# State space's in weights ahead of its out weights, turned between row units; the last product's rests moved from GpSimd to VectorE

## The chip, the cores and the metric

The kernel runs on one NeuronCore of a Trainium2 chip. The metric is the device time of one execution in microseconds (us). Engines are named as the profile names them: PE (TensorE, with PEld for its weight loads), DVE (VectorE), ACT (ScalarE), POOL (GpSimd) and SP (SyncE, which here only issues DMAs). SBUF is the on-chip memory, PSUM the memory that PE writes; DVE and ACT read PSUM, POOL does not.

## What is computed

Two transformer blocks on one sequence of 512 tokens with 1024 features, in fp32. The first block mixes three branches (sparse attention, a gated recurrence, a latent attention) and ends in a feed-forward layer. The second block, in which the change lies, is this, cut to what matters:

```python
def s5_mixer(u, a_re, a_im, log_dt, b_re, b_im, c_re, c_im, d_skip):
    lam_bar = exp(complex(a_re, a_im) * dt)
    b_bar = ((lam_bar - 1) / lam)[..., None] * complex(b_re, b_im)
    # per group of 16 features: 64 complex states
    #   s[t] = lam_bar * s[t-1] + b_bar @ u[t];  y[t] = real(c @ s[t])
    return y + d_skip * u

def hybrid_layer(x, c, ...):
    h = rms_norm(x, norm_g) * (1 + scale) + shift
    proj = h @ w_in          # q, compressed/selected/window keys and values, z_a, gates, u, z_s
    attn = nsa_attention(...) * silu(z_a)        # 8 heads, three branches
    y = gelu(s5_mixer(u, ...))
    y = y * sigmoid(y @ glu_w + glu_b)
    mix = concatenate([attn, y * silu(z_s)]) @ w_out
    return x + gate * mix
```

## The kernel before

One program drives five engines, each with its own list of instructions, kept together by counting semaphores. The order on each engine is the order in which the code writes it; nothing is scheduled later. Names such as `at("in weights 0 3")` are values of such a counter.

**Weights** come from HBM in chunks of up to 128x2048 through `ring`, a ring of four slots. SP issues the loads in a fixed order, each behind the wait that its slot has been used. A *unit* is one output tile of a projection: a feature unit has eight products of 128x512 (each shows as two records), a row unit eight products with 256 columns, or 24 in the last four of the 20 row units. A unit writes one of three PSUM banks (`gemm_bank`), from which ACT copies it (`drain`); PE may take a bank again once the unit three places before was drained. The state space's products go to two other banks (`turn_bank`, `turn0` and `turn1`), which DVE reads.

**Precise products** (`triple`) split each operand into a rounded head and a rest. ACT makes the head of a weight piece (`weight_heads`, into `heads`, four pieces of 128x1024), and another engine subtracts it to get the rest (`ring_r`, in place). In the whole kernel this is DVE (`weight_rests`), but for the last product, `w_out` of the second block (`WOUT2`), it is POOL: its rests of the weights, of the state space's output (`split ssm`) and of three of four key blocks of the attention output (`split late 0` to `2`); DVE makes only the last, `split late 3`.

**State space.** The scan over 512 tokens is done in steps of four tokens (`STEP`), for 16 tiles j of 128 states. Two matrices, real and imaginary (z), hold the loaded weights and their multiples by the decay: `BK` (in weights, lives in `tiles`) and `CK` (out weights, in `rows` and `heads`). DVE folds a factor into `CK` (`fold_out_weights`, 6 instructions), makes four further out weights (24), three in weights (18), clears `TOEP` and makes the diagonal of `d_skip` in the place of the scratch tile `wi`; then `ssm matrices` is reached. PE then multiplies in and out weights (L1106, L1107, four banks, `out weights`), and transposes `BK` in eight groups of four (L1114), which ACT drains back over it as `BT` (`in weights z b4`). ACT also issues three DMAs that spread `TOEP` (L1667), and makes sines and cosines (`waves`, L1653 to L1655). For each of four blocks b4, PE multiplies `BT` with the input `U4` (L1125, `full bu`), DVE turns, scans and turns back (L2386 is the scan) and says `states`, and PE makes y (L1139 to L1141), to which ACT applies the gelu (L1659). Between these steps PE runs `SIDE[b4]` units. SP rearranges `u` into `U4` by 16 DMAs, and y by 16 DMAs (L623) behind `y_done`; the latter stand in its list between the loads of the second and third compression chunks (`cmp_k1`, `cmp_k2`), and the load of `cmp_k1` waits until the second last pair of feature units has been used. The gated linear product (`glu`) waits for them.

**The pair loop.** 64 items of attention (2 branches x 4 query blocks x 8 heads), two to a round p of 32. In round p PE makes the scores of pair p (L1244, L1247), the sums of pair p - 2 (L1270) and the transposes of pair p - 1 (L1256). DVE takes the maximum of pair p (L2578), copies the transposed probabilities of pair p - 1 to `probs` or `probsT` (L1810), and in every second round scales the sums (L2547, L2552). ACT makes the exponentials (L1706). The query blocks have 128, 256, 384 and 512 keys, so rounds 12 to 15 and 28 to 31 are the long ones. After the loop come the halves of the last product (`wide_half`, L707), of which the first ones stand between the last sums, and then four full tiles.

## Time and profile before

| what | value |
|---|---|
| median of three runs | 1583.59 us (1580.87 to 1591.41) |
| profiled execution | 1581.13 us |
| its span, first to last instruction | 1579.3 us |
| mean granted clock of PE | 0.945 of full |
| PE busy | 1423.6 us (90%) |
| DVE busy | 955.5 us (60%) |
| ACT busy | 525.4 us (33%) |
| POOL busy | 83.4 us (5%) |

The profile is of one execution. Its own time is 1.8 us longer than its span, which is what lies around the instructions. Times in the rows are counted from the start of the span. PE's records overlap a little, since products are pipelined, so the distance from start to start is the better measure of what one costs.

### The profile page before, as it was taken

How to read it: one execution, taken by the hardware profiler on the slowest of the kernel's cores; microseconds unless marked ns; L12 is line 12 of the kernel's file. 1: busy time of each engine (PE TensorE's matmuls, PEld its weight loads, DVE VectorE, ACT ScalarE, POOL GpSimd, SP SyncE). 2: the span in 40 equal slices, each digit the busy share in tenths (PEclk: the TensorE clock that was granted, in tenths of full speed). 3: DMA queues.
4: the chain of work that ended last, by engine and by line, in shares of the span. 5: the costliest groups of instructions: out<-in, count | busy, mean ns of one | idle time of the engine just before them, and what ended most of it. 6: DMA issues, size and time to landing. Idle time of an engine off the chain costs nothing.

```text
span 1579.3 us, 18880 instructions
## 1 busy us (share of the span) xinstructions
PE 1423.6 (90%) x7109; PEld 1105.4 (70%) x7110; DVE 955.5 (60%) x1606; ACT 525.4 (33%) x840; POOL 83.4 (5%) x67
## 2 busy tenths in 40 slices
PE   5998888896989877899899999999798999988898
PEld 4758788785567645787688888888557954565576
DVE  6249767676166777774545655533393738868761
ACT  5247332331323554233333333423223031214421
POOL 0000000000000350000000000000000002001212
PEclk9999999997989979899899999999898999989999
DMA  5112111121222120452134444223421122430001
GB/s 229 71 41 93 67 41 54 61 90 47 86 107 81 48 71 14 150 212 92 70 111 183 161 159 155 72 91 110 134 57 63 54 80 72 168 107 1 1 1 54
DMA packets 39882, 140.52 MB, mean 89 GB/s; under 512 B 13040, under 2 KB 17520, under 8 KB 27248
## 3 DMA queue, kind: packets, MB, share of 16 engines
q1 hardware_dynamic: 34608, 130.53, 23.5%
q10 hardware_dynamic: 5184, 8.78, 1.5%
q8 instruction: 57, 0.93, 0.2%
q14 instruction: 33, 0.27, 0.1%
HBM read 128.42 MB, written 8.39 MB: 87 GB/s over the span
## 4 chain that ended last, share of the span: by engine, by line
PE 54%; DVE 4%; ACT 1%; issue 1%; ACTq 0%; DVEq 0%
PE turn L707 24%; PE score L692 7%; PE score L707 7%; PE sum L692 4%; PE sum L707 2%; PE sum L1270 2%; PE score L1244 1%; PE sum L1152 1%; PE score L1152 1%; PE turn L1256 1%; PE turn L829 1%; DVE stat L2578 1%; PE turn L1125 1%; DVE probs L1810 0%; PE score L1206 0%
## 5 line engine op out<-in xcount | busy, mean ns | idle before, releaser
L1852 DVE TENSOR_TENSOR ring_r<-ring,heads_r 128x1024 fp32r<-128x1024 f32 (+3 forms) x153 | 176.3, 1152 | 220.5 <-ACT heads_r L1378 185.0
L1378 ACT ACTIVATE heads_r<-ring 128x1024 fp32r<-128x1024 f32 (+3 forms) x161 | 161.8, 1005 | 250.7 <-DMA ring<-wstream 114.3
L707 PE MATMUL score<-h_sb_r,heads_r 128*128 128x512 f32 x408 | 163.9, 402 | 0.0
L707 PE MATMUL turn<-tiles_r,heads_r 128*128 128x512 f32 x368 | 144.6, 393 | 0.0
L707 PE MATMUL turn<-h_sb_r,heads_r 128*128 128x512 f32 x336 | 132.1, 393 | 8.1 <-DVE ring_r L1852 8.1
L707 PE MATMUL turn<-wide_r,heads_r 128*128 128x512 f32 x312 | 121.9, 391 | 0.0
L707 PE MATMUL turn<-wide_r,ring_r 128*128 128x512 f32 x312 | 121.6, 390 | 0.0
L707 PE MATMUL score<-x_sb_r,heads_r 128*128 128x512 f32 x256 | 109.3, 427 | 8.2 <-DVE ring_r L1852 5.7
L707 PE MATMUL score<-x_sb_r,ring_r 128*128 128x512 f32 x256 | 103.5, 404 | 0.0
L707 PEld LDWEIGHTS score<-h_sb_r,heads_r 128*128 128x128 f32 x408 | 79.5, 195 | 15.1 <-issue 0.5
L707 PEld LDWEIGHTS turn<-tiles_r,heads_r 128*128 128x128 f32 x368 | 70.1, 190 | 14.5
L707 PEld LDWEIGHTS turn<-h_sb_r,heads_r 128*128 128x128 f32 x336 | 63.8, 190 | 21.7 <-issue 8.4
L2630 POOL TENSOR_TENSOR stat<-stat,cst 128x4 f32<-128x4 f32 (+4 forms) x7 | 16.1, 2294 | 1179.7 <-DVE stat L1855 803.9
L707 PE MATMUL sum<-h_sb_r,heads_r 128*128 128x512 f32 x168 | 67.6, 402 | 0.0
L707 PEld LDWEIGHTS turn<-wide_r,ring_r 128*128 128x128 f32 x312 | 58.8, 189 | 12.4
L707 PEld LDWEIGHTS turn<-wide_r,heads_r 128*128 128x128 f32 x312 | 58.9, 189 | 12.2
L707 PEld LDWEIGHTS score<-x_sb_r,heads_r 128*128 128x128 f32 x256 | 50.7, 198 | 22.8 <-issue 10.0
L707 PE MATMUL turn<-h_sb_r,ring_r 128*128 128x512 f32 x160 | 63.0, 394 | 0.0
L707 PEld LDWEIGHTS score<-x_sb_r,ring_r 128*128 128x128 f32 x256 | 50.5, 197 | 11.3
L1706 ACT ACTIVATE tiles<-score,stat 128x128 f32<-128x128 f32 (+3 forms) x64 | 33.7, 527 | 73.3 <-issue 63.2
L692 PE MATMUL score<-h_sb,ring 128*128 128x512 f32 x128 | 55.8, 592 | 0.0
L1347 ACT ACTIVATE tiles<-score 128x512 f32<-128x512 f32 x39 | 24.3, 622 | 91.6 <-PE score L692 41.9
(401 smaller groups left out, 2963.4 us busy)
## 6 DMA issues: line engine op xcount, KB each, us to landing
ring<-wstream SPq DMA_DIRECT2D x95, 1024.0 KB, 4.9
ring<-wstream SPq DMA_DIRECT2D x16, 704.0 KB, 4.3
ring<-gated SPq DMA_DIRECT2D x6, 1024.0 KB, 6.9
gated<-tiles ACTq DMA_DIRECT2D x15, 256.0 KB, 2.0
gated<-probs ACTq DMA_DIRECT2D x9, 256.0 KB, 2.0
x_sb<-xT SPq DMA_DIRECT2D x4, 512.0 KB, 5.6
x_sb<-xT ACTq DMA_DIRECT2D x1, 2048.0 KB, 8.1
outT<-x_sb SPq DMA_DIRECT2D x1, 2048.0 KB, 6.3
```

The costliest lines, as they stand in the source:

```text
L692: mm = pe.matmul(out, l, r, start=(i == 0), stop=(i == len(pairs) - 1))
L707: return pe.matmul(out, a, w, **k) if moving else pe.matmul(out, w, a, **k)
L829: mm = pe.transpose(b[0:src.shape[1], dst:dst + r], src, ident[0:r, 0:r])
L1125: mm = pe.matmul(b[:, jj * P:(jj + 1) * P], BT[z][:, j, :], U4[:, j, :], start=True, stop=True)
L1152: mm = pe.matmul(b[0:2 * NCMP, 0:256], CB[kv][:, 8 * i + l, :], w[:, l, :], start=(i + l == 0), stop=(8 * i + l == 31))
L1244: pe.matmul(PAIR_OF(p)[:, e * T:e * T + cols], TL[r, 18 + j, n * P:(n + 1) * P], KT2[r, 2 * a_ + j // 2, 0:cols], start=True, stop=False)
L1270: mm = pe.matmul(OUT[g][:, h % 4 * P:h % 4 * P + P], PROBT(i)[:, j * P:(j + 1) * P], R2[:, j, at_v:at_v + P], start=(j == 0), stop=(j == n))
L1347: step(act.activation(out, b, func, bias=bias, scale=scale), name, gemm_done)
L1378: step(act.activation(head_piece(p), chunk(name)[:, c:c + cols], ACT.Identity), f"head {p}")
L1706: step(act.activation(PROB(i)[:, 0:cols], PAIR_OF(p)[:, i % 2 * T:i % 2 * T + cols], ACT.Exp, bias=stat[:, 8 + i % 4:9 + i % 4], scale=1.0 ...
L1852: step(dve.tensor_tensor(out, a, b, op), name)
L2630: step(pool.tensor_tensor(v, v, half.broadcast_to([P, n]), ALU.pow), f"rstd {name}")
```

## The change

Seven edits in the state space, and three in the last product.

- DVE makes the three in weights first (`in matrices`), then the fold, the out weights, the clearing of `TOEP` and the diagonal, which gets a place of its own (`SSM_D`, in `prow`).
- PE transposes the eight groups of in weights between the first eight row units (`IN_TURNS`: one unit, one group), real and imaginary in turn, and ACT drains them so.
- The out-weight products come behind the first state product (`out_weights`). `BK` has been overwritten by then, so they read a second copy of the loaded in weights, `B0`, which SP loads by two more DMAs of 128x512.
- ACT drains the out weights and issues the three DMAs of `TOEP` within block 0, behind the first waves and ahead of the second.
- `SIDE`, the units between the state products, becomes 3, 5, 6, 3 (from 5, 5, 5, 4), so that with the eight ahead five feature units are left behind the last y instead of two.
- DVE's wait for the out weights ahead of its first state step goes, as does PE's for POOL.
- DVE makes the rests of the state space's output in rounds 12 to 15 of the pair loop, those of the first four weight pieces in rounds 28 to 31, those of the attention output in rounds 28, 30 and 32 as one 128x4x128 instruction each (POOL used four of 128x128), and those of the last four pieces ahead of its four additions. POOL makes none.

```diff
-    SIDE = [5, 5, 5, 4]
+    SIDE = [3, 5, 6, 3]
+    IN_TURNS = [(z, b4) for b4 in range(4) for z in range(2)]
...
+    B0 = [v.rearrange("p (j c) -> p j c", j=16) for v in (cst[:, coff["reset"][0]:coff["reset"][1]], part(wide, 4200, T))]
+    SSM_D = prow[:, :].bitcast(F32)
...
+                    for z in range(2):
+                        sp.dma_start(B0[z], ssm[:, z * T:(z + 1) * T].rearrange("p (j c) -> p j c", j=16)).then_inc(b0_in, 16)
...
-            run(units, 9)
-            pe.wait_ge(dve_step, at("ssm matrices"))
-            for b4 in range(4):
+            pe.wait_ge(dve_step, at("in matrices"))
+            for z, b4 in IN_TURNS:
+                run(units, 1)
                 b = gemm_bank()
                 for jj in range(4):
...
+                    mm = pe.transpose(b[:, jj * P:(jj + 1) * P], BT[z][:, 4 * b4 + jj, :], ident)
...
+            def out_weights():
+                pe.wait_ge(dve_step, at("ssm matrices"))
+                pe.wait_ge(b0_in, 32)
...
+                            pe.matmul(dst, B0[z][:, j, :], CK[z][:, j, 0:STEP, :], start=(z == 0), stop=False)
...
+                    if b4 == 0:
+                        out_weights()
                     run(units, SIDE[b4])
...
-                        pe.wait_ge(pool_step, at(f"split ssm {k - 4}"))
+                        pe.wait_ge(dve_step, at(f"split ssm {k - 4}"))
...
-            for _ in range(13):
+            for _ in range(4):
+                next(units)
+            for z, b4 in IN_TURNS:
                 next(units)
+                drain(BT[z][:, 4 * b4:4 * b4 + 4, :], f"in weights {z} {b4}", src=lambda g: g[:, :].rearrange("p (j n) -> p j n", j=4))
+            waves(0)
             for b4 in range(4):
+                if b4 == 0:
+                    for k in range(4):
+                        drain(TOEP[0:32, 4 * k:4 * k + 4, :], "out weights" if k == 3 else None,
+                              src=lambda g: g[0:32, :].rearrange("p (j c) -> p j c", j=4))
+                    for m in range(1, STEP):
+                        act.dma_start(TOEP[32 * m:32 * m + 32, :, 32 * m:], TOEP[0:32, :, 0:P - 32 * m]).then_inc(toep_in, 16)
+                    waves(1)
...
-            fold_out_weights()
-            next_out_weights(0)
-            next_out_weights(1)
-            next_out_weights(2)
-            next_out_weights(3)
+            dve.wait_ge(ssm_in, 64)
             for a in (3, 2, 1):
                 next_in_weights(a)
+            tally.named["in matrices"] = tally.count[dve_step.name]
+            fold_out_weights()
+            for a in range(4):
+                next_out_weights(a)
...
+            def attention_rest(n):
+                cols = slice(n * P, (n + 1) * P)
+                dve.wait_ge(act_step, at(f"head attn T {n}"))
+                tt(tiles_r[:, 6 * T:10 * T].rearrange("p (k t) -> p k t", k=4)[:, :, cols], TL[:, 6:10, cols],
+                   WIDE_HEAD[:, 0:4, cols].bitcast(F32), ALU.subtract, f"split late {n}")
...
+                if p in (12, 13, 14, 15):
+                    split(f"ssm {p - 12}", TL[:, p - 10, :], WIDE_HEAD[:, p - 8, :], WIDE_REST[p - 8])
+                if 28 <= p < 32:
+                    weight_rests()
+                if p in (28, 30, 32):
+                    attention_rest((p - 28) // 2)
...
+            attention_rest(3)
             for j in range(4):
+                weight_rests()
                 dve.wait_ge(score_full, at(f"full wout2 {j}"))
```

The new lines push the line numbers of the changed kernel 7 to 24 up: L692 is L699 there, L1114 is L1110, L1125 is L1137, L1852 is L1867, L1810 is L1825, L2578 is L2597.

On PE, from the last two of the four first feature units (128x512) on, the list before reads as follows; `cst` with `tiles` is a group of transposes, `score` and `sum` are the gemm banks, and the products with 256 columns are row units.

```order
L692 MATMUL score<-h_sb,ring 128x512 x16
L692 MATMUL sum<-h_sb,ring 128x512 x8
L692 MATMUL score<-ring,h_sb 128x256 x16
L692 MATMUL sum<-ring,h_sb 128x256 x8
L692 MATMUL score<-ring,h_sb 128x256 x16
L692 MATMUL sum<-ring,h_sb 128x256 x8
L692 MATMUL score<-ring,h_sb 128x256 x16
L692 MATMUL sum<-ring,h_sb 128x256 x8
L1106 MATMUL score<-rows,tiles 32x128
```

and in the changed kernel, from the same place:

```order
L699 MATMUL score<-h_sb,ring 128x512 x16
L699 MATMUL sum<-h_sb,ring 128x512 x8
L699 MATMUL score<-ring,h_sb 128x256 x8
L1110 MATMUL score<-cst,tiles 128x128 x4
L699 MATMUL sum<-ring,h_sb 128x256 x8
L1110 MATMUL score<-cst,tiles 128x128 x4
L699 MATMUL score<-ring,h_sb 128x256 x8
L1110 MATMUL sum<-cst,tiles 128x128 x4
L699 MATMUL score<-ring,h_sb 128x256 x8
L1110 MATMUL score<-cst,tiles 128x128 x4
```

The transposes moved from behind nine row units and the out weights to places between the first eight row units.

On PE, around the first state product (L1125, then L1137), before:

```order
L1114 MATMUL score<-cst,tiles 128x128 x8
L1114 MATMUL sum<-cst,tiles 128x128 x4
L1125 MATMUL turn<-tiles 128x128 x8
L692 MATMUL score<-ring,h_sb 128x256 x16
L692 MATMUL sum<-ring,h_sb 128x256 x8
L692 MATMUL score<-ring,h_sb 128x256 x16
L1125 MATMUL turn<-tiles 128x128 x8
```

and in the changed kernel, where the second fence takes up behind the out weights' last rows:

```order
L1110 MATMUL score<-cst,tiles 128x128 x4
L1137 MATMUL turn<-tiles 128x128 x8
L1124 MATMUL score<-rows,cst 32x128
L1124 MATMUL score<-heads,wide 32x128
L1125 MATMUL score<-prow,cst 32x32
```

```order
L1125 MATMUL score<-prow,cst 32x32
L699 MATMUL sum<-ring,h_sb 128x256 x8
L699 MATMUL score<-ring,h_sb 128x256 x16
L1137 MATMUL turn<-tiles 128x128 x8
L699 MATMUL sum<-ring,h_sb 128x256 x8
```

The out-weight products now stand between the first state product and three row units, where five row units stood alone; they read `cst` and `wide` (the copy `B0`) in the place of `tiles`.

On DVE, rounds 28 to 30 of the pair loop, before; a TENSOR_REDUCE is the maximum of a round, the copies with 512 columns are those of round 29 and 30:

```order
L2578 TENSOR_REDUCE stat<-score 128x2
L1810 COPY probsT<-turn 128x384 x2
L2578 TENSOR_REDUCE stat<-score 128x2
L1810 COPY probs<-turn 128x512 x2
L2547 RECIPROCAL stat<-stat 128x4
L1852 TENSOR_TENSOR stat<-stat,wide 128x4
L2552 TENSOR_TENSOR wide<-sum,stat 128x256
L1852 TENSOR_TENSOR work<-work,wide 128x256
L2578 TENSOR_REDUCE stat<-score 128x2
L1810 COPY probsT<-turn 128x512 x2
```

and in the changed kernel:

```order
L2597 TENSOR_REDUCE stat<-score 128x2
L1825 COPY probsT<-turn 128x384 x2
L1867 TENSOR_TENSOR ring_r<-ring,heads_r 128x1024
L1867 TENSOR_TENSOR tiles_r<-tiles,h_sb_r 128x4x128
L2597 TENSOR_REDUCE stat<-score 128x2
L1825 COPY probs<-turn 128x512 x2
L1867 TENSOR_TENSOR ring_r<-ring,heads_r 128x1024
L2559 RECIPROCAL stat<-stat 128x4
L1867 TENSOR_TENSOR stat<-stat,wide 128x4
L2564 TENSOR_TENSOR wide<-sum,stat 128x256
L1867 TENSOR_TENSOR work<-work,wide 128x256
L2597 TENSOR_REDUCE stat<-score 128x2
```

A weight rest and an attention rest now stand between the copies of round 28 and the maximum of round 29, and a weight rest behind the copies of round 29.

## Rows read from the trace of the kernel before

**Rows 1.** Page, the chain that ended last, share of the span by engine

```profile
PE 54%; DVE 4%; ACT 1%; issue 1%; ACTq 0%; DVEq 0%
```

**Rows 2.** Time line, PE: start us, us, engine line op out<-in xcount [idle before <-releaser]

```profile
1170.62 7.07 PE L692 MATMUL score<-ring,h_sb 128*128 128x256 f32 x32
...
1210.40 0.60 PE L1114 MATMUL sum<-cst,tiles 128*128 128x128 f32 x4
...
1347.08 7.03 PE L692 MATMUL score<-tiles,ring 128*128 128x512 f32 x16
```

**Rows 3.** Windows, PE alone: stretch, us, PE busy, PEclk, DMA share, GB/s

```profile
1209.91:1225.47 15.56, 8.58 (x52) 0.67 0.13 26
1242.74:1244.52 1.78, 1.78 (x17) 1.00 0.00 0
1253.13:1254.92 1.79, 1.79 (x19) 1.00 0.88 357
1254.92:1262.72 7.80, 7.80 (x43) 0.56 0.10 41
1293.76:1296.44 2.68, 2.68 (x26) 1.00 0.53 156
```

**Rows 4.** Time line, DVE and ACT in the state space

```profile
1148.49 0.69 DVE L1852 TENSOR_TENSOR rows<-heads,stat 128x512 f32<-128x512 f32 x1
...
1183.79 1.76 DVE L2348 MEMSET toep<- 128x2048 f32 x1 [0.49 <-DVE tiles L1852]
...
1225.84 0.69 DVE L1852 TENSOR_TENSOR heads<-turn,work 128x512 f32<-128x512 f32 x1 [25.61 <-PE turn L1125]
...
1216.84 0.60 ACT L1347 ACTIVATE tiles<-sum 128x512 f32<-128x512 f32 x1
```

**Rows 5.** Time line of SP, and DMA issues from 1266 on: KB each, us to landing

```profile
1334.22 10.25 SPq L623 DMA_DIRECT2D tiles<-tiles  x16
...
ring<-wstream SPq DMA_DIRECT2D x9, 1024.0 KB, 4.9
tiles<-tiles SPq DMA_DIRECT2D x16, 64.0 KB, 2.0
```

**Rows 6.** Time line, DVE and PE in the pair loop

```profile
1444.76 0.90 DVE L1852 TENSOR_TENSOR stat<-stat,wide 128x4 f32<-128x4 f32 x1
...
1478.09 0.16 DVE L1852 TENSOR_TENSOR stat<-stat,wide 128x4 f32<-128x4 f32 x1
...
1478.74 0.42 DVE L1852 TENSOR_TENSOR work<-work,wide 128x256 f32<-128x256 f32 x1
...
1483.22 2.56 DVE L1852 TENSOR_TENSOR work<-work,wide 128x256 f32<-128x256 f32 x1
...
1487.02 1.70 PE L1270 MATMUL sum<-wide,probsT 128*128 128x128 f32 x8 [2.01 <-DVE probsT L1810]
...
1492.05 1.15 DVE L1852 TENSOR_TENSOR stat<-stat,wide 128x4 f32<-128x4 f32 x1
```

**Rows 7.** Time line, DVE in rounds 29 to 33 and behind them

```profile
1513.70 1.41 DVE L1810 COPY probs<-turn 128x512 f32<-128x512 f32 x2 [0.62 <-PE turn L1256]
...
1521.68 1.42 DVE L1810 COPY probs<-turn 128x512 f32<-128x512 f32 x2 [1.04 <-PE turn L1256]
...
1533.11 0.42 DVE L2552 TENSOR_TENSOR wide<-sum,stat 128x256 f32<-128x256 f32 x1 [5.64 <-PE sum L1270]
...
1537.93 0.69 DVE L1852 TENSOR_TENSOR tiles_r<-tiles,h_sb_r 128x512 fp32r<-128x512 f32 x1 [0.83 <-ACT h_sb_r L1382]
```

**Rows 8.** Groups by shape: DVE's weight rests, whole span; copies, 1448.7 to 1466

```profile
L1852 DVE TENSOR_TENSOR ring_r<-ring,heads_r 128x1024 fp32r<-128x1024 f32 x119 | 145.8, 1225 | 151.1 <-ACT heads_r L1378 115.9 <-ACT trig L1539 32.5
...
L1810 DVE COPY probs<-turn 128x512 f32<-128x512 f32 x4 | 2.8, 692 | 1.8 <-PE turn L1256 1.7
```

**Rows 9.** Windows in the pair loop, all engines (the column behind POOL's is PEclk)

```profile
1487.00:1491.00 4.00, 3.87 (x18) 2.93 (x20) 1.98 (x5) 3.84 (x10) 2.54 (x2) 0.57 0.00 0
...
1496.00:1502.20 6.20, 5.52 (x32) 3.91 (x32) 4.46 (x9) 3.81 (x9) 4.35 (x5) 0.72 0.00 0
```

More of the change, by code:

```diff
@@ L702, in triple @@
                     split_seen.add(p)
-                    pe.wait_ge(pool_step if p >= WOUT2 else dve_step, at(f"split {p}"))
+                    pe.wait_ge(dve_step, at(f"split {p}"))
                 wh, wr = head_piece(p)[:, c - c0:c - c0 + n], chunk(name, ring_r)[:, c:c + n]
@@ L1113, in _ @@
                     for jj in range(4):
-                        mm = pe.transpose(b[:, jj * P:(jj + 1) * P], BT[z][:, 4 * b4 + jj, :], ident)
+                        j = 4 * b4 + jj
+                        dst = b[0:32, jj * P:(jj + 1) * P]
+                        for z in range(2):
+                            pe.matmul(dst, B0[z][:, j, :], CK[z][:, j, 0:STEP, :], start=(z == 0), stop=False)
+                        mm = pe.matmul(dst[:, 0:32], ident[:, 0:32], by_tile(SSM_D)[:, b4, jj * 32:jj * 32 + 32], start=False, stop=True)
                     mm.then_inc(gemm_full, 1)
@@ L1320, in _ @@
             for n in range(NT):
-                pe.wait_ge(dve_step if n == NT - 1 else pool_step, at(f"split late {n}"))
+                pe.wait_ge(dve_step, at(f"split late {n}"))
             for e in range(4):
@@ L1659, in gelu @@
                 step(act.activation(TL[:, 2 + b, :], O[0][:, :], ACT.Gelu_apprx_tanh), f"y gelu {b}", y_done)
-            for _ in range(13):
+            for _ in range(4):
                 next(units)
+            for z, b4 in IN_TURNS:
+                next(units)
+                drain(BT[z][:, 4 * b4:4 * b4 + 4, :], f"in weights {z} {b4}", src=lambda g: g[:, :].rearrange("p (j n) -> p j n", j=4))
+            waves(0)
             for b4 in range(4):
-                drain(TOEP[0:32, 4 * b4:4 * b4 + 4, :], "out weights" if b4 == 3 else None,
-                      src=lambda g: g[0:32, :].rearrange("p (j c) -> p j c", j=4))
-            for m in range(1, STEP):
-                act.dma_start(TOEP[32 * m:32 * m + 32, :, 32 * m:], TOEP[0:32, :, 0:P - 32 * m]).then_inc(toep_in, 16)
-            for z in range(2):
-                for b4 in range(4):
-                    drain(BT[z][:, 4 * b4:4 * b4 + 4, :], f"in weights {z} {b4}", src=lambda g: g[:, :].rearrange("p (j n) -> p j n", j=4))
-                    if z == 0 and b4 < 2:
-                        waves(b4)
-            for b4 in range(4):
+                if b4 == 0:
[5 more added lines that the diff above has]
+                    waves(1)
                 if b4 >= 2:
@@ L2340, in _ @@
             take_turn(None, rstd_final)
-            fold_out_weights()
-            next_out_weights(0)
-            next_out_weights(1)
-            next_out_weights(2)
-            next_out_weights(3)
+            dve.wait_ge(ssm_in, 64)
             for a in (3, 2, 1):
                 next_in_weights(a)
+            tally.named["in matrices"] = tally.count[dve_step.name]
+            fold_out_weights()
+            for a in range(4):
+                next_out_weights(a)
             step(dve.memset(TOEP, 0.0))
-            tt(cols32("wi"), con("same").unsqueeze(1).broadcast_to([P, 16, 32]), over(sm("ssm_d")), ALU.mult, "ssm matrices")
+            tt(SSM_D.rearrange("p (j c) -> p j c", j=16), con("same").unsqueeze(1).broadcast_to([P, 16, 32]), over(sm("ssm_d")), ALU.mult, "ssm matrices")
             def phases(b):
@@ L2374, in _ @@
                 dve.wait_ge(turn_full, m + 2)
-                if b == 0:
-                    dve.wait_ge(gemm_done, at("out weights"))
                 tt(wr, br, c_, ALU.mult)
```

30 lines of the change are left out of this document (1 added, 29 removed).

## The prediction

> **What bounds the kernel now.** I read three views in this order. The chain of waits comes first: it gives TensorE (PE) 54% of the span and VectorE (DVE) 4% [rows 1], so work taken from another engine is worth time only where PE waits for it. Then I read the time line of PE from the end of the first block to the end, looking for PE's own idle time, and the windows beside it for PE's granted clock. The stretch that matters runs from the first row unit of the second block, which begins at 1170.62, to the gated linear product, which begins at 1347.08: 176.5 us [rows 2]. Within it PE stands still at one place for long. The eight groups of turned in weights and the first state product, 1209.91 to 1225.47, take 15.56 us with PE busy for 8.58 of them, at a clock of 0.67 [rows 3]: each group needs a gemm bank, and ScalarE (ACT), which empties the banks, is meanwhile issuing three DMAs and making two tables of waves. From there to 1347.08 PE only waits once, about 2 us, for the third gelu. DVE is not the limit there: it waits 25.61 us for the first product of the state space [rows 4].
>
> The other stretch is the loop over 32 pairs of heads and the last product, 1396.5 to 1541.5. There PE, DVE and ACT hand work round, and GpSimd (POOL) makes the rests.
>
> **Part one, the state space.** The in weights now come first on DVE. They are the last 18 of 48 equal instructions that took from 1148.49 to 1183.30 before (the clearing of TOEP starts 0.49 behind them [rows 4]), 0.73 us each, 13.1 in all; they now begin when the fold began and end at 1161.6, so PE, which reaches them at 1170.62, does not wait. Fold, out weights, the clearing of TOEP and the diagonal follow in the same total, so "ssm matrices" stays near 1186, and PE asks for it only after 1203.
>
> Eight groups of four transposes now lie between eight row units of 3.45 us. A group that does not wait costs PE 0.49 us, from the 1209.91 at which the first began to the 1210.40 at which the second did [rows 2, 3]. Eight are 3.9 us. ACT empties a bank of them in 0.60 us [rows 4] and gets one every 2 us, so no bank is late. PE reaches the first state product at 1170.62 + 8 x (3.45 + 0.49) = 1202.1. The first state product now follows a stretch without a gap, so I give it the 1.78 us that the second took at full clock [rows 3]. Both together: 15.56 - 3.9 - 1.8 = **9.9 us less**, of which the product is 0.9. The out weights follow it, 8.1 us of PE as before; their four banks outrun ACT, which makes the first waves then, by one bank at most. The two loads of the B0 copy are 256 KB each behind four loads on SP's queue, 9 us before the next chunk is asked for: nothing.
>
> The other units only change places around the four state products. DVE begins its states some 20 us earlier, which lies beside PE's work and pays nothing by itself. Two things could take the gain back. First, PE's clock: it fell to half during the units of 24 columns, and 1254.92 to 1262.72 took 7.80 us where the same kinds of work took 1.79 and 2.68 at full clock, 3.3 us lost [rows 3]. Those four units now stand in one row, followed by wide units, so I take the same loss again. Second, the rearranging of y: 16 DMAs that SP issues in 10.25 us, each landing 2.0 us later [rows 5], so 12.3 us from first to last. SP may only begin once it has issued the load of the second compression chunk, which waits for the second last pair of feature units. After that pair PE has two units left, each with the 16 products of 128x512 that the last of [rows 2] has, 6.87 us from start to start: 13.7 us. The other condition, y_done, is met 20 us earlier. The margin is 1.4 us; it holds. The part: **9.9 us less**.
>
> **Part two, the rests of the last product.** DVE takes over four rests of the state space output (0.69 us, like the one it already makes for the last keys [rows 7]) in rounds 12 to 15, four weight rests (1.225 us [rows 8]) in rounds 28 to 31, three attention rests of 0.69 in rounds 28, 30 and 32, and four weight rests in the last product. With the gap behind each instruction I count 0.73 and 1.26.
>
> What goes: POOL's instructions lengthen DVE's. A 128x4 product takes 0.16 us and took 0.90 and 1.15; a 128x256 one takes 0.42 and took 2.56, while a POOL subtraction ran [rows 6]. The three are 0.74, 0.99 and 2.14 us, and behind the last PE waited 2.01 [rows 6]; I take 0.74 + 0.99 + 2.01 = **3.7 us less** (bounds 0 and 3.9, the three in full). The Trainium skill gives the mechanism ("SBUF — State Buffer", section "Who interferes with whom"): a DVE instruction with two SBUF inputs and a GpSimd one that reads SBUF exclude each other for the whole instruction. The trace agrees in its 2.56 us. By the rule every such meeting would block fully, and the sum would keep its size, since most of DVE's work in the loop reads PSUM.
>
> What comes, rounds 12 to 15: 4 x 0.73 = 2.9 us, each behind copies that wait for PE; the copies of both kinds there wait about 3.5 us in all, 1.8 of them on the probabilities [rows 8]. I take 0, bounds 0 and 2.9. Rounds 28 to 31: before the maximum of round 31 DVE now has three weight rests and two attention rests more, 3 x 1.26 + 2 x 0.73 = 5.2 us. It was idle 0.62 us in front of the copy at 1513.70 and 1.04 in front of the copy at 1521.68 [rows 7], and those waits fill first: 5.2 - 0.6 - 1.0 = **3.6 us more**, all of it on PE, whose sums wait for these copies. The fourth weight rest and the third attention rest are covered: PE then works on the last product, and DVE waited 5.64 us for it [rows 7]. Bounds: 0 if PE's own slack takes it, and 4 x 1.26 + 3 x 0.73 = 7.2 if every one counts. In the final product the four rests are ready at about 1544 to 1552 while PE needs the first at 1549.75, and DVE's additions wait for PE anyway: 0. Cover gone, one rest would cost 1.26. The part: 3.6 - 3.7 = **0.1 less**.
>
> **The sum**: 9.9 + 0.1 = 10.0 us less. The profiled execution took 1581.1 us (span 1579.3), so 1571.1. The median of the three runs is 2.5 above it, so beside the median the same difference gives 1573.6. I take 1573.
>
> **Rivals.**
> 1. *The clock stays up, 0.17.* The 3.3 us above do not come back, and neither do the two stretches in the loop at 0.57 for 4.0 us and 0.72 for 6.2 [rows 9], which began behind PE's waits for DVE; they cost 1.7 + 1.7. Then 6.7 us less again: 1566. Against it: in the first stretch PE was busy all the time and the clock still fell [rows 3]. The Trainium skill says the opposite would hold ("TensorE: Matmul & The Clock Gate", section "What's actually happening"): a PE that has been busy is granted the full clock. By that rule this rival is the forecast; the row speaks against it, since 7.80 busy us of 7.80 had 0.56.
> 2. *DVE becomes the bound of the loop, 0.15.* All added work counts, 2.9 and 7.2 where I have 3.6: 6.5 more, 1579.5. For it: after the added work DVE has hardly an idle row left in rounds 28 to 31. Against: its waits for PE in rounds 12 to 15 [rows 8].
> 3. *PE waits for y at the gated product, 0.10.* The chunk's load (4.9 us [rows 5]) goes right ahead of the 16 DMAs, and should it hold them up in full, PE waits 4.9 - 1.4 = 3.5: 1577.
> 4. *The turns are not hidden, 0.08.* If each unit's bank is late by one emptying, 8 x 0.6 = 4.8: 1578. So the change would not do what it says. Against: ACT has nothing else to do in the eight rounds.
> 5. *Slower: PE's clock falls in the eight rounds, 0.05.* Transposes between units at every 3.9 us leave the array less filled. At half clock the rounds and the out weights, 31 + 8 us, take that much longer: 1573 + 39 = 1612. It decides once 10 us are lost, which is 20 us spent at half clock. Against: the state products between units at 1242.74 had 1.00 [rows 3].
>
> **How the numbers follow.** The forecast holds 0.45. A measurement of this kernel tells about 1% from no change, 15.8 us. Faster by more: rival 1 and a few of the forecast's cases, 0.21. Slower by more: rival 5, 0.05. Within: the rest, 0.74. The range reaches down past rival 1 and up past rivals 2 to 4: 1565 to 1581; rival 5 and the far ends of the costs are left out.
>
> **What the changed profile would show.** Right: the transposes between row units, with no wait of PE for ACT's tiles; the last pair of in weights before 1203; PE at the gated product near 1337; no DVE product of 128x256 over 0.5 us from 1440 to 1541; PE waiting 3 to 4 us for DVE's copies in rounds 29 to 32. Wrong: a wait in front of the gated product or the state products, clocks under 1 in the eight rounds, or waits in rounds 12 to 16. Most likely to upset the number is where the clock falls in the loop of pairs, since its phase moves with everything ahead.

## The result, and the profile after

The changed kernel takes **1573.92 us** (median of 13 runs, 1569.24 to 1579.56), the kernel before 1582.59 (13 runs beside them, 1580.41 to 1591.41): ratio 0.9945, 95% interval 0.9929 to 0.9960, so 8.7 us less (6.3 to 11.2). The profiled execution took 1573.08 us, its span is 1571.3, the mean granted clock of TensorE 0.949.

Time line of PE in the changed kernel: the first row unit, the first two groups of transposes, the four narrow row units (24 columns) with the feature unit behind them, the fourth y, and the gated linear product.

```profile
1171.39 3.62 PE L699 MATMUL score<-ring,h_sb 128*128 128x256 f32 x16
1174.84 0.60 PE L1110 MATMUL score<-cst,tiles 128*128 128x128 f32 x4
1175.28 3.62 PE L699 MATMUL sum<-ring,h_sb 128*128 128x256 f32 x16
1178.74 0.60 PE L1110 MATMUL score<-cst,tiles 128*128 128x128 f32 x4
...
1246.50 1.86 PE L699 MATMUL score<-ring,h_sb 128*128 128x24 f32 x16
1248.21 2.64 PE L699 MATMUL sum<-ring,h_sb 128*128 128x24 f32 x16
1250.67 7.00 PE L699 MATMUL score<-ring,h_sb 128*128 128x24 f32 x32
1257.50 9.80 PE L699 MATMUL sum<-h_sb,ring 128*128 128x512 f32 x16
...
1303.93 0.80 PE L1153 MATMUL sum<-tiles,toep 128*128 128x128 f32 x2 [2.02 <-ACT tiles L1673]
...
1342.64 3.60 PE L699 MATMUL score<-tiles,ring 128*128 128x512 f32 x8
```

A group costs 0.44 us (1174.84 to 1175.28). From the first row unit to the gated product it is 171.25 us, where [rows 2] have 176.46. That is 5.2 less, and not 9.9. The windows of PE say where the rest is: stretch, us, busy, granted clock.

```profile
1171.39:1202.53 31.14, 31.14 (x162) 1.00 0.26 72
1202.53:1204.41 1.88, 1.88 (x19) 1.00 0.45 105
1204.41:1212.52 8.11, 8.11 (x97) 1.00 0.26 107
1246.50:1257.50 11.00, 11.00 (x66) 0.63 0.01 3
1257.50:1267.13 9.63, 9.63 (x17) 0.72 0.31 109
1303.93:1308.30 4.37, 4.37 (x24) 0.62 0.00 0
```

Of a stretch in which PE is always busy, length x (1 - clock) is what the clock lost: 4.1 + 2.7 + 1.7 = 8.4 us, where [rows 3] have 7.80 x 0.44 = 3.4. 6.8 us of it lie in the four narrow units and the feature unit behind them, which take 20.63 us at 0.67; the 1.7 us behind the fourth y are another loss, behind PE's wait of 2.02 us. The row units with the transposes, the first product and the out weights ran at full clock.

SP, behind the load of the second compression chunk:

```profile
1329.10 0.33 SPq L650 DMA_DIRECT2D ring<-wstream  x1
1329.47 10.26 SPq L630 DMA_DIRECT2D tiles<-tiles  x16
```

The last of the 16 lands about 2.0 us behind 1339.7 [rows 5], 0.9 us ahead of the gated product, which doesn't wait.

In the pair loop, PE's waits and the compressed scores (L1220), answering to [rows 6, 7]:

```profile
1405.61 3.68 PE L1220 MATMUL score<-rows,tiles 128*128 128x64 f32 x32
...
1440.23 0.98 PE L1230 MATMUL turn<-cst,heads 128*128 128x128 f32 x4 [2.25 <-DVE probsT L1825]
...
1460.81 1.13 PE L1239 MATMUL turn<-tiles,heads 128*128 128x256 f32 x4 [0.80 <-DVE probsT L1825]
...
1485.63 1.17 PE L1284 MATMUL sum<-wide,probsT 128*128 128x128 f32 x8 [0.29 <-DVE probsT L1825]
...
1504.43 2.02 PE L1284 MATMUL sum<-wide,probs 128*128 128x128 f32 x16 [0.66 <-DVE probs L1825]
1509.63 2.05 PE L1284 MATMUL sum<-wide,probsT 128*128 128x128 f32 x16 [1.03 <-DVE probsT L1825]
1514.33 0.65 PE L836 MATMUL turn<-cst,work 128*128 128x128 f32 x4 [1.77 <-DVE probs L1825]
```

The wait of 2.01 us [rows 6] is gone (a smaller one of 0.58 us, at 1480.98 here, stands a few instructions behind its place, where the kernel before has none), and DVE's products of the later rounds take what they should:

```profile
1483.05 0.16 DVE L1867 TENSOR_TENSOR stat<-stat,wide 128x4 f32<-128x4 f32 x1
1483.70 0.42 DVE L1867 TENSOR_TENSOR work<-work,wide 128x256 f32<-128x256 f32 x1
```

Three waits in rounds 29 to 32 have come, 3.46 us (one of them was there before with 0.44 us). The windows of the loop, PE alone: its entrance with the compressed scores, the next 50 us, and the rest up to the last product.

```profile
1395.20:1409.29 14.09, 12.10 (x90) 0.88 0.08 33
1409.29:1459.29 50.00, 41.78 (x284) 0.93 0.00 1
1459.29:1517.40 58.11, 49.86 (x362) 1.00 0.00 1
```

In the third of them the clock is full; the kernel before had the two low stretches of [rows 9] there.

The difference of the two spans, 8.0 us, by stretches from start to start: 0.8 more ahead of the first row unit, where PE's list is the same in both; 5.2 less to the gated product; none to the loop; 0.7 more from there to the compressed scores; 3.3 less in these, which ran at half clock before (6.93 us) and at full clock after (3.68); 1.1 less from there to the last product; 0.1 more behind.

### The profile page after: what moved, and what is told of

The parts are those of the page before. It is cut to its first block, busy times and chain, and to the rows that moved or that the text cites. A ratio compares the mean times of both kernels' runs of the same rounds, so it can differ in the third digit from the quotient of the medians.

```text
span 1571.3 us, 18872 instructions
## 1 busy us (share of the span) xinstructions
PE 1421.7 (90%) x7109; PEld 1103.0 (70%) x7110; DVE 965.8 (61%) x1621; ACT 525.4 (33%) x840; POOL 52.7 (3%) x43
## 4 chain that ended last, share of the span: by engine, by line
PE 53%; DVE 5%; issue 1%; ACT 1%; DVEq 0%; ACTq 0%
PE turn L714 24%; PE score L699 7%; PE score L714 7%; PE sum L699 5%; PE sum L714 2%; PE sum L1284 1%; PE sum L1166 1%; PE score L1166 1%; DVE stat L2597 1%; DVE probs L1825 1%; PE score L1258 1%; PE turn L836 1%; PE turn L1270 1%; DVE probsT L1825 1%; PE turn L1137 0%
## 5 line engine op out<-in xcount | busy, mean ns | idle before, releaser
L1867 DVE TENSOR_TENSOR ring_r<-ring,heads_r 128x1024 fp32r<-128x1024 f32 (+3 forms) x161 | 186.1, 1156 | 228.7 <-ACT heads_r L1392 193.0
L699 PE MATMUL score<-h_sb,ring 128*128 128x512 f32 x128 | 55.9, 592 | 0.0
```

The lines of the kernel that those rows point to most:

```text
L699: mm = pe.matmul(out, l, r, start=(i == 0), stop=(i == len(pairs) - 1))
L1867: step(dve.tensor_tensor(out, a, b, op), name)
```

## The experiments

Each ran beside the kernel before. Differences from it are ratios of its runs, with the 95% interval. Stretches are from one profiled execution: "to the gated product" is counted from the start of the first row unit, 176.46 before and 171.25 after. A second profile of the changed kernel (experiment 9) has 169.66 there, so a difference of 1.6 us between two kernels in this stretch can be one of executions. Experiment 12 ran before 6, 9, 10 and 11.

**1. Part one alone** (`p1_only`): the rests go back to GpSimd, written as before.

```diff
-                    pe.wait_ge(dve_step, at(f"split {p}"))
+                    pe.wait_ge(pool_step if p >= WOUT2 else dve_step, at(f"split {p}"))
...
```

> The state space's edits alone; the rests stay with GpSimd as before. The prediction's own terms give 9.9 us less than before (about 1572.7 beside the median of 1582.6). Reading the profile after, I now expect 5.2 us less at the start of the gated linear product (171.3 us behind the first row unit in the place of 176.5), since the four narrow row units in one row and the two units behind them run at half clock. What the pair loop does then tells two theories apart: if the full clock that the compressed scores had in the profile after (3.7 us in the place of 6.9) came with part one, the whole is 8.5 to 9.5 less, about 1573.5; if it came with the rests of part two, 5.2 less, about 1577.4.

Measured: 1577.04 us, ratio 0.9976 (0.9961 to 0.9991), 3.8 less. To the gated product 169.66: 6.8 less. The four narrow units and the feature unit behind them took 20.62 us at a clock of 0.67, 6.8 us lost, as in the changed kernel. The compressed scores took 6.93 us, at half clock. So part one is worth 3.8 us (1.4 to 6.2) by the runs and 5.0 by the two profiled spans, without the full clock at the compressed scores. The wait of 2.01 us [rows 6] is still there with 2.00, and so is the low clock behind it:

```profile
1483.00:1493.00 10.00, 8.99 (x44) 0.66 0.01 2
```

**2. Part two alone** (`p2_only`): the kernel before with VectorE's rests, without GpSimd's.

```diff
+                if p in (12, 13, 14, 15):
+                    split(f"ssm {p - 12}", TL[:, p - 10, :], WIDE_HEAD[:, p - 8, :], WIDE_REST[p - 8])
+                if 28 <= p < 32:
+                    weight_rests()
+                if p in (28, 30, 32):
+                    attention_rest((p - 28) // 2)
...
```

> The rests of the last product by VectorE alone; the state space stays as before. The prediction's sum: 3.6 more in rounds 28 to 31, 3.7 less where GpSimd no longer lengthens VectorE's instructions, so 0.1 less, about 1582.5. If VectorE were the bound of the loop it would be 6 us slower, 1589. If the low clock at the compressed scores and behind round 22 came from GpSimd's work, it would be 3 to 6 us faster, 1577 to 1580. In the trace I expect no wait of TensorE near the place of the 2.01 us one, three waits of 0.7, 1.0 and 1.8 us in rounds 29 to 32, and the compressed scores still at half clock.

Measured: 1580.36 us, ratio 0.9991 (0.9978 to 1.0005), so 1.4 less (3.5 less to 0.8 more). The time line of PE:

```profile
1412.17 6.93 PE L1206 MATMUL score<-rows,tiles 128*128 128x64 f32 x32
...
1512.40 2.02 PE L1270 MATMUL sum<-wide,probs 128*128 128x128 f32 x16 [0.66 <-DVE probs L1810]
1517.61 2.05 PE L1270 MATMUL sum<-wide,probsT 128*128 128x128 f32 x16 [1.04 <-DVE probsT L1810]
1522.30 0.66 PE L829 MATMUL turn<-cst,work 128*128 128x128 f32 x4 [1.77 <-DVE probs L1810]
```

The three waits are those of the changed kernel to 0.01 us, and the 2.01 is gone, as expected. The low stretches of [rows 9] are gone too:

```profile
1469.10:1494.10 25.00, 22.09 (x154) 1.00 0.01 1
1494.10:1525.37 31.27, 26.70 (x202) 1.00 0.00 1
```

From the compressed scores to the last product it took 106.27 us with PE busy for 90.87 of them, the kernel before 109.21 with 93.67. So PE's idle time is the same to 0.1 us (15.4 for 15.5), as the prediction's sum has it, and 2.8 of the 2.9 us gained are the clock's. The profiled span is no shorter all the same (1579.2 for 1579.3), since the first row unit begins at 1173.43, 2.8 us later than in the profile before. The full clock at the compressed scores was there in neither of these two profiles; experiment 9 shows that a kernel can have it in one execution and not in the next.

The two parts alone give 3.8 + 1.4 = 5.2 us, together 8.7. The intervals are wide enough for this difference of 3.5 us to be chance, and no run explains it.

**3. Two pairs of narrow units** (`narrow_split`).

```diff
-    SIDE = [3, 5, 6, 3]
+    SIDE = [3, 7, 4, 3]
```

> The changed kernel with SIDE 3, 7, 4, 3 in the place of 3, 5, 6, 3: two of the four row units with 24 columns stand ahead of the first y and the third state product, two behind them, where all four stood in a row. If the clock falls because narrow products stand together, less is lost: the profile after has 11.0 us at a clock of 0.63 and 9.6 at 0.72 there, about 6.8 us over full clock; with two pairs I expect half of it or none, so 3 to 7 us less at the gated product, 1567 to 1571. If any two narrow units cost what four do, the low stretch comes twice or stays as long: no change, 1574.

Measured: 1571.81 us, ratio 0.9932 (0.9915 to 0.9949). To the gated product 164.67, 6.6 less than the changed kernel. Windows of PE on the second narrow unit, the first y behind it, and the second pair with the feature unit behind:

```profile
1245.62:1247.41 1.79, 1.79 (x19) 1.00 0.92 352
1247.41:1251.80 4.39, 4.39 (x27) 0.61 0.19 80
1253.58:1264.03 10.45, 10.45 (x51) 1.00 0.31 102
```

Only the first y lost clock, 1.7 us (it takes 2.68 at full clock [rows 3]). The time is only 2.1 us under the changed kernel's, less than the 3 to 7 expected: this profile is of an execution of 1568.41, and the median lies 3.4 above it. Where the other runs lose it no profile shows.

**4. Each narrow unit followed by a feature unit** (`narrow_apart`).

```diff
+            def in_turn(narrow, wide):
+                for _ in narrow:
+                    yield
+                    next(wide)
+                    yield
...
-            units = itertools.chain(*[row_units(f"rows2_{n}", width(parts), H) for n, parts in ROWS2], first)
+            narrow = row_units("rows2_g", 24, H)
+            units = itertools.chain(*[row_units(f"rows2_{n}", width(parts), H) for n, parts in ROWS2[:-1]], in_turn(narrow, first), first)
...
```

ACT's drains are put in the same order.

> The changed kernel with each of the four row units with 24 columns followed by one feature unit; same units, same number of places. With four in one row the profile after lost 6.8 us in them and the two units behind; with two pairs 1.7 us, all in the products of the first y. If it takes a row of narrow units to bring the clock down, a single one between wide units costs nothing and the gated product starts 163 us behind the first row unit (171.3 after, 164.7 with two pairs): 8 less than the changed kernel, 1566. If one narrow unit does it too, each costs 1 to 2 us and it lands at 167 to 171: 1570 to 1574.

Measured: **1566.0 us** (4 runs, 1565.59 to 1566.81), ratio 0.9893 (0.9872 to 0.9913). To the gated product 163.04, 8.2 less than the changed kernel (6.6 less than its second profile), and no clock lost from the narrow units on, in the window over all four and what stands between them:

```profile
1247.04:1286.13 39.09, 39.09 (x171) 1.00 0.14 54
```

**5. The groups of transposes together** (`turns_together`), behind the eight row units, ahead of the first state product.

```diff
+            run(units, 8)
             for z, b4 in IN_TURNS:
-                run(units, 1)
...
```

ACT's drains are put in the same order.

> The changed kernel with its eight groups of transposes in one row behind the eight row units, ahead of the first state product, in the place of one group behind each unit. All else as in the changed kernel. In the profile after a group costs TensorE 0.44 us, 3.5 in all. By the term of the prediction, a group in a row waits for a bank that ScalarE empties in 0.60 us, so from the fourth group on every group costs at least 0.6: the first state product comes 31.1 + about 1.3 = 32.4 us behind the first row unit. If the order of ScalarE's list (its DMAs and waves stood among the drains before) was what cost the time and not the places between units, this is all: 1 to 2 us more than the changed kernel, 1575. If the places between units carry the gain, the first state product comes 36 us behind or later and the kernel is 5 us or more slower, 1579.

Measured: 1572.60 us, ratio 0.9936 (0.9920 to 0.9951). The first state product comes 31.99 us behind the first row unit, 0.85 later than in the changed kernel; the kernel is not slower. The last groups on PE:

```profile
1199.54 0.66 PE L1110 MATMUL sum<-cst,tiles 128*128 128x128 f32 x4
1200.17 1.28 PE L1110 MATMUL score<-cst,tiles 128*128 128x128 f32 x8
1201.42 0.66 PE L1110 MATMUL sum<-cst,tiles 128*128 128x128 f32 x4
1202.05 0.66 PE L1110 MATMUL score<-cst,tiles 128*128 128x128 f32 x4
1202.55 0.72 PE L1137 MATMUL turn<-tiles 128*128 128x128 f32 x5
```

0.63 us a group, ScalarE's 0.60 for a drain and the gap behind it. The places between the row units are worth 0.85 us here, all the rest of the gain at this spot is elsewhere. That the whole time is no longer also has another reason: the same four narrow units with their feature unit lost half as much clock in this profile, 3.5 us in the place of 6.8:

```profile
1246.52:1263.88 17.36, 17.36 (x82) 0.80 0.17 61
```

**6. The waves back among the drains** (`waves_among`), shown against experiment 5.

```diff
-            for z, b4 in IN_TURNS:
+            for i, (z, b4) in enumerate(IN_TURNS):
                 drain(BT[z][:, 4 * b4:4 * b4 + 4, :], f"in weights {z} {b4}", ...)
-            waves(0)
+                if i < 2:
+                    waves(i)
...
-                    waves(1)
```

> As the kernel with the eight groups together (first state product 31.99 us behind the first row unit, 0.85 later than the changed kernel), but ScalarE makes the tables of waves 0 and 1 behind the first and the second drain of a group, as it did in the kernel before, and not behind the last drain and within block 0. If ScalarE's list was the cost, TensorE waits for the third and fourth bank: 3.3 us for the first waves with their table load and 2.1 for the second, so the first state product comes at 37 to 37.5 and the kernel is about 5 us slower than with the groups together, 1577. If the place of the groups behind the out weights was the cost, it stays at 32 and nothing changes, 1573.

Measured: 1588.38 us (12 runs), ratio 1.0025 (1.0007 to 1.0042), 15.8 over the last. PE at the groups:

```profile
1203.60 0.66 PE L1110 MATMUL sum<-cst,tiles 128*128 128x128 f32 x4
1207.59 0.70 PE L1110 MATMUL score<-cst,tiles 128*128 128x128 f32 x4 [3.33 <-ACT tiles L1361]
1210.30 1.12 PE L1110 MATMUL score<-cst,tiles 128*128 128x128 f32 x4 [2.01 <-ACT tiles L1361]
```

The two waits are the two tables of waves, 5.3 us, and the groups behind them run at half clock; the first state product comes at 38.29, 6.3 later. In the kernel before, the wait of 3.33 us was the same, and a third wait stood ahead of it, behind ScalarE's three DMAs, which this edit does not put back:

```profile
1210.69 2.12 ACTq L1667 DMA_DIRECT2D toep<-toep  x3
...
1213.50 0.66 PE L1114 MATMUL score<-cst,tiles 128*128 128x128 f32 x4 [2.06 <-ACT tiles L1347]
```

From the first group to the end of the first state product it is 6.24 us in experiment 5 and 13.50 here, so the waves are worth 7.3 us at this spot (the product runs at half clock behind them). The 15.56 us before are 2.06 more, the size of that third wait.

The rest of the 15.8 is not in these waits. The two profiled spans differ by 17.6 us: 6.3 here, 4.2 from there to the gated product (4.2 us more of busy PE for the same instructions), 3.0 from the loop's start to the last product, and 4.1 ahead of the first row unit, where PE's list is the same. Ten of the 12 runs lie between 1587.62 and 1590.09, and two at 1577.17 and 1579.12, where the sum of the waits has them. Why most lie 10 us above it is open.

**7. Rests moved out of rounds 28 to 31** (`rests_moved`).

```diff
-                if 28 <= p < 32:
+                if p in (24, 26):
                     weight_rests()
-                if p in (28, 30, 32):
-                    attention_rest((p - 28) // 2)
+                if p == 32:
+                    weight_rests(2)
+                    attention_rest(0)
+                    attention_rest(1)
...
+            attention_rest(2)
             take_attention(3)
```

> The changed kernel with the weight rests of rounds 28 to 31 moved: two to rounds 24 and 26, where VectorE waits for TensorE anyway, two with two attention rests behind the last copies (round 32), the third attention rest behind round 33. If the three waits of TensorE in rounds 29 to 32 (0.66, 1.03 and 1.77 us in the profile after, one of 0.42 before) are the cost of these rests, they fall to about 0.5 in all: 3.0 us less than the changed kernel, 1571. If TensorE only waits for something else there, or the same waits come up in rounds 25, 27 and behind the loop, no change, 1574.

Measured: 1571.17 us (6 runs, 1564.72 to 1578.64), ratio 0.9939 (0.9917 to 0.9961). PE's waits from round 27 on:

```profile
1503.92 0.66 PE L836 MATMUL turn<-cst,work 128*128 128x128 f32 x4 [1.17 <-DVE probs L1825]
1519.87 0.66 PE L836 MATMUL turn<-cst,work 128*128 128x128 f32 x4 [0.44 <-DVE probs L1825]
```

The 3.46 us are 0.44, and a wait in round 27 rose from 0.42 to 1.17: 2.3 less. The runs spread over 14 us, so the time says little here; experiment 10 measures this edit again.

**8. A feature unit ahead of the fourth y** (`y3_unit`).

```diff
+                else:
+                    run(units, 1)
                 if b4 >= 1:
                     i = b4 - 1
...
```

> The changed kernel with one of the five last feature units put between the third and the fourth y. The 2.02 us that TensorE waits there for the third gelu go; so does what the clock loses behind that wait (1.7 us in the profile after, 1.3 to 1.7 in others, none in the profile before). So 2.0 to 3.7 less at the gated product, 1570 to 1572, if nothing else comes late. The fourth y is ready 6.9 us later; if the 16 DMAs of y then wait for it, TensorE waits at the gated product and nothing is gained, 1574.

Measured: 1576.74 us (6 runs, 1575.69 to 1579.10), ratio 0.9960 (0.9945 to 0.9975). The wait is gone, the gated product starts at 167.37, 3.9 earlier (2.3 earlier than in the second profile), and doesn't wait for y; yet the kernel is not faster: its median is 2.8 above the changed one's, 2.4 by the ratios, whose intervals overlap. The windows from the loop's start to the end of the compressed scores, and from there to the last product:

```profile
1391.38:1410.61 19.23, 18.11 (x90) 0.53 0.06 24
1410.61:1520.82 110.21, 93.97 (x643) 0.94 0.00 1
```

The first took 14.09 at 0.88 in the changed kernel (above), the second 108.11: with the same instructions, 5.1 and 2.1 us longer, so more than the 3.9 us was given back there. Beside the second profile of the changed kernel (16.73 and 106.61) it is 6.2 us for 2.3.

**9. The changed kernel again** (`after_again`).

> The changed kernel once more, unchanged, for a second profile of it. What the program fixes should come again to 0.2 us: the first state product 31.14 behind the first row unit, the gated product 52.56 ahead of the loop, three waits of 0.66, 1.03 and 1.77 us in rounds 29 to 32. What the clock decides should not: between the start of the loop and the first half of the last product the first profile lost 5.2 us to the clock, and the kernel with the rests moved, the same program up to round 24, lost 15.1 there. If that loss is chance in each execution, this one has another value and the times spread over 10 us again; if it is fixed by the program, it is 5.2 again.

Measured: 1574.69 us (6 runs, 1572.68 to 1575.57), ratio 0.9940 (0.9920 to 0.9960). First state product at 31.14, gated product at 169.66 (171.25 in the first profile), compressed scores 6.92 us (3.68), the loop's entrance, with 14.09 at 0.88 in the first:

```profile
1395.94:1412.67 16.73, 14.16 (x90) 0.77 0.07 27
```

The three waits are 0.66, 1.03 and 1.77 us again, and from the gated product to the loop it is 52.56 again. So these waits and distances are fixed by the program to 0.1 us. The narrow units with their feature unit are so too, 20.62 us at 0.67; the 1.7 us behind the fourth y are not, they did not come here (2.78 us at full clock). What the clock loses in the loop is not fixed, not even for one kernel, and a wait there can move with it: the one at the loop's entrance that is 0.24 us in the first profile is 0.81 in this one.

**10. Narrow units apart, rests moved** (`apart_rests`: edits 4 and 7).

> The narrow units apart and the rests moved out of rounds 28 to 31, without the feature unit ahead of the fourth y and without the quartered product. The narrow units apart gave 1566.0; the rests moved took the three waits of 0.66, 1.03 and 1.77 away and gave 2.7 less than the changed kernel. Added: 1563. If the loop's clock takes it back, as with the feature unit ahead of the fourth y, where TensorE reached the gated product 3.9 us earlier and the kernel came out 3 slower, 1568 or more.

Measured: **1563.40 us** (5 runs, 1563.11 to 1565.32), ratio 0.9876 (0.9857 to 0.9895): 19.6 less than before by the ratio, the best median of all. From the compressed scores to the last product 108.49 us, 2.51 less than with edit 4 alone, at the same clocks (0.92 and 0.97 in both): the price of the rests in rounds 28 to 31.

**11. With VectorE's long product quartered as well** (`apart_rests_za`).

```diff
-                if p == 7:
+                if p in (16, 17, 18, 19):
...
-                    stt(za4, h_sb[:, 0:4 * T], 1.0, za4, ALU.add, ALU.mult)
+                    stt(za, h_sb[:, (p - 16) * T:(p - 15) * T], 1.0, za, ALU.add, ALU.mult)
```

> As the one before with VectorE's product with the tanh of za quartered and put in rounds 16 to 19. In the profile of the kernel with all edits the wait behind round 7 fell from 3.64 to 1.31, and waits in rounds 17 to 20 rose by 1.1 (1.23 from 0.51, 0.74 from 0.31), with the clock down once more behind them (1.7 us). So 1.2 us less without the clock, 0.5 more with it: 1561.8 to 1563.5. It also tells whether the feature unit ahead of the fourth y was what made the kernel with all edits slow (1567.4): if so this one is 4 us faster than that.

Measured: 1565.05 us (6 runs, 1559.32 to 1565.36), ratio 0.9877 (0.9857 to 0.9896): no gain over the last. It is 2 us under experiment 12, not the 4 expected, so the runs do not tell whether the feature unit ahead of the fourth y is what makes that one slow.

**12. Edits 4, 7, 8 and 11** (`together_n`).

> All edits that the profile speaks for in one kernel: the narrow units apart, a feature unit ahead of the fourth y, the rests moved out of rounds 28 to 31, and VectorE's product with the tanh of za (128x2048, 2.29 us in round 7, behind which TensorE waits 3.64) as four of 128x512 in rounds 16 to 19, where VectorE waits for TensorE. If the terms add up: 8.3 for the narrow units, 2.0 for the third gelu (its clock loss is in doubt), 3.0 for the rests, 2.3 for the product: 15.6 less than the changed kernel, about 1558. If the waits of the loop only shift (as the clock does), half of the last two: about 1561. If the clock finds other places to fall: 1564.

Measured: 1567.36 us, ratio 0.9886 (0.9861 to 0.9910), with runs from 1557.22 to 1568.45 and one of 2864.06, which the ratio leaves out (the five others have a median of 1567.29). One execution reached the 1558 of the sum, the others lie 7 to 10 above it. Its profile (the execution took 1567.29) has the gated product at 160.76, 2.3 ahead of edit 4's, and the entrance of the loop at half clock:

```profile
1395.00:1405.00 10.00, 9.63 (x46) 0.50 0.00 1
```

## Why the prediction held, and where it was off

The number (1573 for 1573.92) held with luck. The forecast was 10.0 us less beside a median of 1583.59 from three runs; the change brought 8.7 beside 1582.59. And the 8.7 are not made up as forecast. In the first profile part one fell 4.7 us short; 2.5 us less from the loop's start to the end of the compressed scores, and 1.1 less (forecast 0.1) from there to the last product, make up for most of that; neither comes from a step of the sum. In the second profile part one fell 3.1 us short, and the loop behind the compressed scores was 2.6 shorter than before.

**Part one, the fixed part: right.** First state product 31.14 us behind the first row unit; the prediction has 31.5 (a group costs 0.44 us for its 0.49, the product 1.88 for 1.78). Where no clock is lost, the gated product comes at 163.04; the forecast's 176.46 - 9.9 with its 3.3 us of clock loss taken out is 163.3. The in weights, the y DMAs (0.9 us of margin for 1.4) and the two B0 loads cost nothing, as said.

**Part one, the step that failed** is "Those four units now stand in one row, followed by wide units, so I take the same loss again". It was 3.3 us and became 6.8, in the changed kernel, in its second profile and with part one alone, though 3.5 in experiment 5; where the clock also fell behind the wait for the third gelu, as in the first profile, 1.7 came on top. The kernel before had three narrow units, then y and a state product, then the fourth. With two pairs the loss is 1.7, and singly it is nothing; this is shown, as is that the order costs 8 us of the whole time (edit 4). Why the chip does so was not tried. Part one brought 5.2 and 6.8 us in the two profiles for 9.9, and alone 3.8 by the ratio.

**The cause of the 15.56 us** was named rightly, ScalarE's list. That the turns had to go between row units for it is not so: together they cost 0.85 us more. Of the 15.56 us, 6.24 are left in experiment 5, 7.3 are the waves (experiment 6), and the 2.06 that remain are the size of the wait behind the three DMAs, for which no edit of its own was run. VectorE's new order (in weights first) serves only the places between units: in experiment 5 all the matrices are made at 1186.1, and the groups begin at 1198.2. That it could go back with them was not tried.

**Part two.** The three meetings with GpSimd are gone nearly as priced: PE's waits went from 2.98 to 2.25, from 2.01 to 0 and from 1.22 to 0.29 us, 3.7 in all, and the new one of 0.58 takes a part of it back, 3.1. Rounds 28 to 31 cost 3.0 us in the waits, and 2.5 by experiment 10, for 3.6: mis-sized by 0.6 to 1.1. The bound of 0 if PE's own slack takes it was too low, and that of 7.2 far too high. Rounds 12 to 15: one wait rose from 0.45 to 0.80, for 0. So the waits named give 0.3 more, and PE's whole idle time from the compressed scores on is 0.1 less with part two alone, 0.9 and 0.2 more in the two profiles of the changed kernel; predicted was 0.1 less. What part two did gain came by the clock: 2.8 us less of busy PE in experiment 2, which the sum leaves to rival 1.

**Rival 1** was half right. The two stretches of [rows 9] did not come back, in the changed kernel nor with part two alone. The rival prices them at 3.4 us; PE's busy time fell by 2.8 in experiment 2. With part one alone, where GpSimd still makes the rests, the wait of 2.00 us was followed by 0.66 over 10 us. At the narrow units the clock did the opposite of the rival. The Trainium skill ("TensorE: Matmul & The Clock Gate", section "What's actually happening") ties the full clock to how busy PE has been. The trace disagrees at the narrow units, 0.63 with PE busy for 11.00 of 11.00 us, and the measurement decides. The same section of the Trainium skill says that where the clock changes differs from run to run. Experiment 9 agrees for the loop; at the narrow units two executions of one kernel have the same 20.63 and 20.62 us.

**The compressed scores** gave 3.3 us that no step had: 6.93 before, 3.68 in the first profile after, 6.92 in the second. So the change doesn't fix it. How often each kernel has it was not measured: of the 14 profiles five have them in 3.6 to 3.9 us from start to start (the first of the changed kernel and experiments 3, 4, 10 and 11), the others in 6.9.

**Rivals 2 to 5** did not occur. VectorE was no bound in rounds 12 to 16, PE waited for nothing at the gated product or for a bank between row units, and the eight rounds ran at 1.00.

**Open.** What sets the clock in the first 70 us of the loop. Up to round 24 the kernel with the rests moved is the changed kernel; its profile took 19.37 us for the loop's entrance, for which the changed one took 14.09 and 16.73. The kernel of experiment 8 reaches the loop earlier, and all its six runs take 1575.69 us or more; so do five of the changed kernel's first 13 and none of its later six. So neither chance nor the edit is shown as the cause.

## What to carry to other kernels

Before moving units to hide a wait, ask whose list made it: two entries of ScalarE's list cost 7 us here, the places of eight groups under one. When units are put in another order, count how many small ones follow each other, since the loss grows with the row (none for one, at most 1.7 us for two, 3.5 to 6.8 for four here); of the 6.8 us, 4.1 lie in them and 2.7 behind them, in wide products. And compare stretches with their granted clock beside them: a few microseconds saved ahead of a stretch in which the clock moves can be given back there, as in experiment 8, though the edit changed nothing in it.

## What was not expected of the hardware

- PE busy without a gap falls to half clock in a row of units of 24 columns (11.00 us at 0.63), and the feature unit behind them takes 9.63 us for 6.87. With a feature unit between them: 39.09 us at 1.00.
- One kernel, two executions: 3.68 and 6.92 us for the same 32 products, at half and at full clock.
- The stretch ahead of the first row unit took 1170.6 to 1174.6 us in the profiles, though PE's list is the same there in all kernels.
